# Ending each projection token tile by token tile, in a 256-token, two-block float32 network on one core

## The chip, the cores and the metric

The kernel runs on one core of a Trainium2 chip. TensorE (PE) multiplies, VectorE (DVE) and ScalarE (ACT) do elementwise work, GpSimd (POOL) helps, and SyncE (SP) issues the loads. The metric is the device time of one execution in microseconds (us). Less is better.

## The reference, cut to what matters

Two residual blocks over x of 256 tokens by 2048 features. In each, a mixer and then a gated feed-forward part:

```python
x = x + rms_norm(mix @ w_out[l], post_mix_norm[l])     # "out1" (block 1), "out2" (block 2)
h = rms_norm(x, pre_ffn_norm[l])
u = causal_dwconv(h @ w_up[l], conv_w[l], conv_b[l])   # "up1", "up2"
gate, up = jnp.split(u, 2, axis=-1)
y = (jax.nn.gelu(gate, approximate=True) * up) @ w_down[l]   # "down1", "down2"
x = x + rms_norm(y, post_ffn_norm[l])
```

`rms_norm` divides a token's row by the root of its mean square over all 2048 features. So no part of x can be updated before the last columns of `mix @ w_out` or `y` are known for that token; another token's columns are not needed.

## The kernel before

Tokens lie on the 128 partitions, in two token tiles t = 0, 1. Each matrix product runs over chunks of weights: a chunk is two blocks of 128 rows by 512 columns. Float32 accuracy comes from splitting both operands in a rounded part and a rest: ACT rounds a chunk of `raw` into `whi` (`split_hi`, L213), DVE subtracts into `wlo` (`split_lo`, L218), and PE makes three products a block and token tile, hi by hi, hi by lo, lo by hi (`products`, L231 to L233). There are four slots (RING) for chunks. A slot is reused when PE has used it (`chunk_used`); ACT and DVE work up to three chunks ahead (LEAD), into the next stage too. The stages follow each other as in1, out1, up1, down1, in2, out2, up2, down2. A stage works in groups of 512 output columns; a group fills one of two pairs of PSUM banks (`acc`), one bank a token tile.

In out1, down1, out2 and down2 the stationary operand is the token data (`ahl` or `hhi`, `hlo`), and the moving one is the weights. In up1 and up2 it is turned about (`products_turned`, L251 and L253): the weights are stationary, `ahl` moves in 512 and in 256 columns, and the group takes `acc` or `tp` banks.

At the end of out and down stages stands a chain, the **boundary** in this text: the last group's columns times the gain go to `ybuf` (DVE, `back_group_dve` L396, out stages L1378 and L1919), ACT squares the bank in place with a row sum into `psq` (`back_group_act` L404), DVE adds up the sums and scales (`post_root_dve` L437, L439), ACT takes the root (L421), DVE the reciprocal (L442), DVE updates x by quarters of 512 columns for both token tiles (`add_rows` L450, in quarters q), PE turns x (`pre_pe` L299, eight 128x128 turns a quarter), ACT and DVE split the turned quarter (`pre_act` L306, `pre_dve` L317) into `ahl`, and the next stage's products can start. Every engine takes its instructions in the order in which they are written for it. In SBUF `whi` and `wlo` start 128 bytes past a multiple of 512; `ybuf`, `hhi`, `hlo` and `ahl` start 384 bytes past one.

Of the kernel before, what the change touches and what calls it, by code (L numbers as in the profile page):

```python
# [55 lines left out]
def bass_two_blocks(nc, T):  # L56
    with ExitStack() as ctx:
# [19 lines left out]
        prs = sb("prs", [P, 4, NT])  # L77
        prime = sb("prime", [P, 1])
# [242 lines left out]
        def lead_pe(pe, ph, c, src, ready):  # L321

            for q in {0: (0, 1), 2: (2,), 4: (3,)}.get(c, ()):
                pre_pe(pe, ph, q, src, ready)
# [6 lines left out]
        def lead_dve(dve, ph, c, gain, source):  # L331

            if c == 3:
                source(0)
                source(1)
                pre_dve(dve, ph, 0, gain)
                source(2)
                pre_dve(dve, ph, 1, gain)
            if c == 4:
                source(3)  # L340
# [29 lines left out]
        def back_pe(pe, ph, xhi, xlo, nch, ready=None, ready_count=None, last_count=None, src=None, src_ready=None):  # L370
            def body(i, first):
                for c in range(2 * nch):
                    if c % nch == 0:
                        group(pe, gb[ph] + c // nch + 2 * i)
                    if first:
                        lead_pe(pe, ph, c, src, src_ready)
                    if last_count and CK * c == 4 * (FG - 1):
                        pe.wait_ge(ready, last_count)
                    products(pe, cb[ph] + c + i * (2 * nch), c % RING, acc[(gb[ph] + c // nch) % 2],
                             xhi, xlo, CK * (c % nch), CK * nch, ph if first and c < nch else None)  # L380
            if src is None:
                pe.wait_ge(ready, ready_count)
                with pe.Fori(0, 2) as i:
                    body(i, False)
            else:
                body(0, True)
                body(1, False)
# [22 lines left out]
        def back_act(act, ph, k, nch, last=False):  # L410
            for i in range(2):
                for c in range(LEAD if i else TAIL_HI, 2 * nch):
# [3 lines left out]
                if not (i and last):  # L416
                    for c in range(2 * nch, 2 * nch + LEAD):
                        s_hi(act, ph, i, 2 * nch, c)
                back_group_act(act, ph, k, i, 1)
            act.wait_ge(sem(f"{ph}_post"), 2)  # L420
            act.activation(prs[:, k, :], prs[:, k, :], ACT.Sqrt).then_inc(sem(f"{ph}_post"), 1)  # L421

        def back_dve(dve, ph, k, nch, gain_row, last=False):
            for i in range(2):
                for c in range(LEAD if i else TAIL_LO, 2 * nch):
# [3 lines left out]
                if not (i and last):  # L429
                    for c in range(2 * nch, 2 * nch + LEAD):  # L430
                        s_lo(dve, ph, i, 2 * nch, c)
                back_group_dve(dve, ph, i, 1, nch, gain_row)
            post_root_dve(dve, ph, k)

        def post_root_dve(dve, ph, k):
            dve.wait_ge(group_free, gb[ph] + NG)
            dve.tensor_reduce(prs[:, k, :], psq[:, k, :, :], AX.X, ALU.add).then_inc(sem(f"{ph}_post"), 1)  # L437
            dve.wait_ge(sem(f"{ph}_post"), 1)
            dve.tensor_scalar(prs[:, k, :], prs[:, k, :], 1.0 / D, EPS, ALU.mult, ALU.add)\  # L439
               .then_inc(sem(f"{ph}_post"), 1)  # L440
            dve.wait_ge(sem(f"{ph}_post"), 3)
            dve.reciprocal(prs[:, k, :], prs[:, k, :]).then_inc(sem(f"{ph}_post"), 1)  # L442
            dve.wait_ge(sem(f"{ph}_post"), 4)

        def add_rows(dve, ph, k):

            def add(q):
                c = slice(q * GC, (q + 1) * GC)
                for t in range(NT):
                    dve.scalar_tensor_tensor(out=x[:, t, c], in0=ybuf[:, t, c], scalar=prs[:, k, t:t + 1],  # L450
                                             in1=x[:, t, c], op0=ALU.mult, op1=ALU.add)\
                       .then_inc(sem(f"{ph}_x"), 1)
            return add

        def x_ready(ph):

            def wait(e, q):
                e.wait_ge(sem(f"{ph}_x"), 2 * q + 2)
            return wait
# [351 lines left out]
        def m1_pe(pe):  # L811
# [232 lines left out]
            for n, (g, q) in enumerate(LAID1):  # L1044
# [14 lines left out]
                between(N1 + n)  # L1059

        def m1_act(act):
# [137 lines left out]
            for n in range(LEAD, N1 + len(LAID1) + LEAD):  # L1199
                if n in (3, 6, 8):  # L1200
                    pre_act(act, "in1", n // 3 if n < 8 else 3, 0)
                s_hi(act, "in1", 0, 0, n)
# [7 lines left out]
            back_group_act(act, "out1", 0, 1, 1)  # L1210
            act.wait_ge(sem("out1_post"), 2)
            act.activation(prs[:, 0, :], prs[:, 0, :], ACT.Sqrt).then_inc(sem("out1_post"), 1)

        def m1_dve(dve):
# [208 lines left out]
            for n in range(LEAD, N1 + len(LAID1) + LEAD):  # L1423
# [18 lines left out]
            out1_group(3)  # L1442
            post_root_dve(dve, "out1", 0)
# [62 lines left out]
        def m2_pe(pe):  # L1506
# [80 lines left out]
            for n in range(len(LAID2)):  # L1587
# [12 lines left out]
                between(N2 + n)  # L1600

# [34 lines left out]
        def m2_act(act):  # L1636
# [103 lines left out]
            for n in range(len(LAID2) + LEAD):  # L1740
# [7 lines left out]
                else:  # L1748
                    s_hi(act, "up2", 0, 0, n - len(LAID2))
# [4 lines left out]
            back_group_act(act, "out2", 2, 1, 1)  # L1754
            act.wait_ge(sem("out2_post"), 2)
            act.activation(prs[:, 2, :], prs[:, 2, :], ACT.Sqrt).then_inc(sem("out2_post"), 1)

        def m2_dve(dve):
# [137 lines left out]
            for n in range(len(LAID2) + LEAD):  # L1896
# [5 lines left out]
                if n < len(LAID2):  # L1902
                    s_lo(dve, "out2", 0, 0, n)
                else:
                    s_lo(dve, "up2", 0, 0, n - len(LAID2))
# [4 lines left out]
            out2_group_dve(dve, 3)  # L1910
            post_root_dve(dve, "out2", 2)
# [16 lines left out]
        def _(sp):  # L1928
# [8 lines left out]
            for q in range(4):  # L1937
# [22 lines left out]
        def _(pe):  # L1960
# [3 lines left out]
            back_pe(pe, "down1", hhi, hlo, DCH, sem("up1_hid"), FG, FG + 1)  # L1964
            m2_pe(pe)
            up_pe(pe, "up2", x_ready("out2"))
            back_pe(pe, "down2", hhi, hlo, DCH, sem("up2_hid"), FG, FG + 1)

        @block.scalar
        def _(act):  # L1970
# [3 lines left out]
            back_act(act, "down1", 1, DCH)  # L1974
            m2_act(act)
            up_act(act, "up2", 1, sem("out2_x"), 8)
            back_act(act, "down2", 3, DCH, last=True)

        @block.vector
        def _(dve):  # L1980
# [3 lines left out]
            back_dve(dve, "down1", 1, DCH, gbd)  # L1984
            m2_dve(dve)
            up_dve(dve, "up2", 1, add_rows(dve, "out2", 2))
            back_dve(dve, "down2", 3, DCH, gbd, last=True)
            for q in range(4):
                add_rows(dve, "down2", 3)(q)
# [53 lines left out]
```

## Time and profile before

| | us |
|---|---|
| median of 3 runs | 2558.8 |
| the three runs | 2558.58, 2566.81, 2558.8 |
| profiled execution, its own time | 2559.84 |
| span of the profiled execution | 2557.6 |
| PE busy | 2511.5 (98%) |
| DVE busy | 1653.1 (65%) |
| ACT busy | 1333.7 (52%) |

The span runs from the first to the last instruction; 2.2 us of the execution's time lie around it. PE's busy time counts overlapping matmuls from their modelled ends, so it tells that PE hardly ever waits and not that it works at its peak.

### The profile page before, as it was taken

What the parts mean: (1) busy time and instruction counts of PE and PEld (TensorE: products, weight loads), DVE (VectorE), ACT (ScalarE), POOL (GpSimd) and SP (SyncE); (2) the same over time, 40 slices, a digit from 0 to 9 for tenths busy, and PEclk for the clock granted to TensorE, in tenths of its full rate; (3) what the DMA queues carried; (4) which work ended last, traced back from release to release, by engine and by line L of the source; (5) the groups of instructions that cost most, each with busy time, mean ns of one, the idle gap of its engine ahead of it and who ended that gap; (6) DMA issues with size and microseconds to landing.
All of it is one profiled execution on the core that took longest, in us unless ns stands there. A gap on an engine that the chain in (4) does not pass through costs nothing.

```text
span 2557.6 us, 40519 instructions
## 1 busy us (share of the span) xinstructions
PE 2511.5 (98%) x15344; PEld 2155.9 (84%) x15344; DVE 1653.1 (65%) x2014; ACT 1333.7 (52%) x1749; POOL 222.2 (9%) x94
## 2 busy tenths in 40 slices
PE   8999999999999999999999999999999999999997
PEld 8999877888888888887888888888788888888886
DVE  5665674677677775445485868775676676775444
ACT  5454564656556554444645455554555656554442
POOL 1000000022121211000000000000012131221000
PEclk9999999999999999999999999999999999999999
DMA  7865345566666666665655655546566666656664
GB/s 223 250 205 157 113 127 178 152 190 187 195 190 189 187 191 204 199 191 172 189 174 165 175 157 172 164 145 195 156 181 192 185 186 185 186 181 214 189 190 146
DMA packets 241791, 462.11 MB, mean 181 GB/s; under 512 B 14344, under 2 KB 23361, under 8 KB 241169
## 3 DMA queue, kind: packets, MB, share of 16 engines
q1 hardware_dynamic: 240001, 453.44, 58.7%
q0 software_dynamic: 1568, 7.10, 0.9%
q8 instruction: 77, 1.26, 0.2%
q14 instruction: 33, 0.27, 0.0%
q10 hardware_dynamic: 112, 0.03, 0.0%
HBM read 458.40 MB, written 2.12 MB: 180 GB/s over the span
## 4 chain that ended last, share of the span: by engine, by line
PE 98%; DVE 1%; ACT 1%; issue 0%; DMA 0%; SPq 0%; DVEq 0%; ACTq 0%
PE acc L231 13%; PE acc L233 13%; PE acc L232 13%; PE acc L251 13%; PE tp L251 13%; PE tp L253 7%; PE acc L253 7%; PE acc L828 3%; PE acc L830 2%; PE acc L831 2%; PE acc L1055 1%; PE acc L1057 1%; PE acc L1056 1%; PE tp L299 1%; PE tp L1535 1%; PE acc L836 1%
## 5 line engine op out<-in xcount | busy, mean ns | idle before, releaser
L218 DVE TENSOR_TENSOR wlo<-raw,whi 128x1024 fp32r<-128x1024 f32 x856 | 1070.8, 1258 | 761.6 <-ACT whi L213 759.8
L213 ACT ACTIVATE whi<-raw 128x1024 fp32r<-128x1024 f32 x856 | 903.3, 1059 | 1017.0 <-PE acc L233 467.5
L251 PE MATMUL acc<-ahl,whi 128*128 128x512 f32 x1408 | 495.1, 396 | 0.0
L251 PE MATMUL tp<-ahl,whi 128*128 128x512 f32 x1408 | 494.2, 395 | 0.0
L253 PE MATMUL acc<-ahl,wlo 128*128 128x256 f32 x1408 | 395.0, 281 | 0.0
L253 PE MATMUL tp<-ahl,wlo 128*128 128x256 f32 x1408 | 394.9, 280 | 0.0
L251 PEld LDWEIGHTS acc<-ahl,whi 128*128 128x128 f32 x1408 | 264.3, 188 | 62.3 <-issue 0.4
L251 PEld LDWEIGHTS tp<-ahl,whi 128*128 128x128 f32 x1408 | 263.9, 187 | 61.8
L231 PE MATMUL acc<-whi,ahl 128*128 128x512 f32 x768 | 305.7, 398 | 0.0
L233 PE MATMUL acc<-whi,ahl 128*128 128x512 f32 x768 | 299.9, 390 | 0.0
L232 PE MATMUL acc<-wlo,ahl 128*128 128x512 f32 x768 | 299.5, 390 | 0.0
L232 PE MATMUL acc<-wlo,hhi 128*128 128x512 f32 x704 | 274.0, 389 | 0.0
L231 PE MATMUL acc<-whi,hhi 128*128 128x512 f32 x704 | 274.0, 389 | 0.0
L233 PE MATMUL acc<-whi,hlo 128*128 128x512 f32 x704 | 274.0, 389 | 0.0
L253 PEld LDWEIGHTS acc<-ahl,wlo 128*128 128x128 f32 x1408 | 266.5, 189 | 0.0
L253 PEld LDWEIGHTS tp<-ahl,wlo 128*128 128x128 f32 x1408 | 266.2, 189 | 0.1
L631 POOL TENSOR_TENSOR cvg<-cvg,cvu 128x1024 f32<-128x1024 f32 x22 | 98.0, 4456 | 1516.5 <-DVE cvu L575 1516.5
L233 PEld LDWEIGHTS acc<-whi,ahl 128*128 128x128 f32 x768 | 144.4, 188 | 31.0
L231 PEld LDWEIGHTS acc<-whi,ahl 128*128 128x128 f32 x768 | 144.4, 188 | 29.8 <-issue 0.2
L232 PEld LDWEIGHTS acc<-wlo,ahl 128*128 128x128 f32 x768 | 144.6, 188 | 28.6
L232 PEld LDWEIGHTS acc<-wlo,hhi 128*128 128x128 f32 x704 | 132.1, 188 | 27.6
L233 PEld LDWEIGHTS acc<-whi,hlo 128*128 128x128 f32 x704 | 132.1, 188 | 27.5
(251 smaller groups left out, 2902.5 us busy)
## 6 DMA issues: line engine op xcount, KB each, us to landing
raw<-in_w_up_dram SPq DMA_DIRECT2D x176, 512.0 KB, 4.0
raw<-in_ffn_w_in_dram SPq DMA_DIRECT2D x176, 512.0 KB, 3.8
raw<-in_hgrn_w_in_dram SPq DMA_DIRECT2D x160, 512.0 KB, 3.6
raw<-in_w_in_dram SPq DMA_DIRECT2D x88, 512.0 KB, 3.7
raw<-in_w_down_dram SPq DMA_DIRECT2D x88, 512.0 KB, 3.9
raw<-in_ffn_w_out_dram SPq DMA_DIRECT2D x88, 512.0 KB, 3.7
raw<-in_w_out_dram SPq DMA_DIRECT2D x32, 512.0 KB, 3.7
raw<-in_hgrn_w_out_dram SPq DMA_DIRECT2D x32, 512.0 KB, 3.9
```

Of the source, the lines that this page charges most:

```text
L213: act.activation(whi[:, s, :], raw[:, s, :], ACT.Copy).then_inc(hi_done, 1)
L218: dve.tensor_tensor(wlo[:, s, :], raw[:, s, :], whi[:, s, :].bitcast(F32), ALU.subtract).then_inc(lo_done, 1)
L231: pe.matmul(out[:, t, :], xh, whi[:, s, c], start=(kt == 0), stop=False)
L232: pe.matmul(out[:, t, :], xh, wlo[:, s, c], start=False, stop=False)
L233: mm = pe.matmul(out[:, t, :], xl, whi[:, s, c], start=False, stop=(kt == nk - 1))
L251: pe.matmul(o[:, ct % 2, :].rearrange("p (a t) -> p a t", a=2), whi[:, s, c], ahl[:, :, kt, :], start=(kt == 0), stop=False, skip_group_ch ...
L253: mm = pe.matmul(o[:, ct % 2, 0:S], wlo[:, s, c], ahi[:, kt, :], start=False, stop=(kt == KT - 1), skip_group_check=True)
L299: mm = pe.transpose(tp[q % 2][:, k, t * P:(t + 1) * P], src[:, t, c:c + P], ident[:, :])
L631: pool.tensor_tensor(cvg[:, :, :], cvg[:, :, :], cvu[:, :, :], ALU.mult).then_inc(sem(f"{ph}_pr"), 1)
L828: pe.matmul(o[:, d], whi[:, s, a], ahi[:, kt, :], start=first and ct % 2 == 0, stop=False, skip_group_check=True)
L830: pe.matmul(o[:, d], whi[:, s, a], alo[:, kt, :], start=False, stop=False, skip_group_check=True)
L831: mm = pe.matmul(o[:, d], wlo[:, s, a], ahi[:, kt, :], start=False, stop=last, skip_group_check=True)
```

## The change

Four edits, at all four boundaries.

1. The last four chunks of an out or down stage are multiplied for token tile 0 first and then for tile 1 (`last_products`); a semaphore `token0` tells when tile 0 is whole. `back_pe` is written out where it was a loop of two passes.
2. Norm and additions go by token tile. DVE sums the squares of the first three groups ahead (`rest_dve`), ACT squares a tile's last 512 columns out of the bank into the other pair of banks and takes the root with scale and bias in the same instruction (`last_act`), DVE makes the reciprocal, then updates x a quarter and tile at a time, with the last group's `ybuf` (`last_y`) and two chunks of `wlo` of the next stage in between (`last_dve`). The three `whi` of the next stage stand between tile 0 and tile 1 on ACT.
3. PE turns quarters 0 and 1 of x by token tile (`pre_pe_by_token`), and in up1 and up2 ahead of the wait for the banks. After down2 the output goes out as one transfer for tile 0 and four for tile 1.
4. A tensor `rest` (32 bytes a partition) and 96 bytes of padding come in, so that `ybuf`, `hhi`, `hlo` and `ahl` start at a multiple of 512 bytes. `whi` and `wlo` stay 128 bytes past one.

```diff
+        rest = sb("rest", [P, 4, NT])
+        sb("pad128", [P, 24])
...
+        def pre_pe_by_token(pe, ph, src, ready):
+
+            for t in range(NT):
+                for q in range(2):
+                    ready(pe, q, t)
+                    for k in range(4):
+                        c = (4 * q + k) * P
+                        mm = pe.transpose(tp[q][:, k, t * P:(t + 1) * P], src[:, t, c:c + P], ident[:, :])
+                    if t == NT - 1:
+                        mm.then_inc(sem("pre_turned"), 1)
...
             if c == 3:
-                source(0)
-                source(1)
                 pre_dve(dve, ph, 0, gain)
-                source(2)
+                s_lo(dve, ph, 0, 0, 2)
+                for t in range(NT):
+                    source(2, t)
                 pre_dve(dve, ph, 1, gain)
...
+        def last_products(pe, ph, k, n, xhi, xlo, kts):
+
+            out = acc[(gb[ph] + NG - 1) % 2]
+            for t in range(NT):
+                for j in range(RING):
+                    if t == 0:
+                        pe.wait_ge(lo_done, n + j + 1)
+                    s = (n + j) % RING
+                    for kk in range(CK):
+                        kt, c = kts[j] + kk, slice(kk * GC, (kk + 1) * GC)
+                        xh, xl = xhi[:, kt, t * P:(t + 1) * P], xlo[:, kt, t * P:(t + 1) * P]
+                        pe.matmul(out[:, t, :], xh, whi[:, s, c], start=False, stop=False)
+                        pe.matmul(out[:, t, :], xh, wlo[:, s, c], start=False, stop=False)
+                        mm = pe.matmul(out[:, t, :], xl, whi[:, s, c], start=False, stop=(j == RING - 1 and kk == CK - 1))
+                    if t:
+                        mm.then_inc(chunk_used, 1)
+                if t == 0:
+                    mm.then_inc(sem("token0"), 1)
+
+        def last_act(act, ph, k, t, end):
...
+            act.activation(other[:, t, :], a[:, t, :], ACT.Square, accum_out=psq[:, k, t, NG - 1:NG])\
+               .then_inc(sem("last_sq"), 1)
+            act.wait_ge(sem("last_sq"), NT * k + t + 1)
+            act.wait_ge(sem("rest"), 2 * k + 2)
+            act.activation(prs[:, k, t:t + 1], psq[:, k, t, NG - 1:NG], ACT.Sqrt, scale=1.0 / D,
+                           bias=rest[:, k, t:t + 1]).then_inc(sem("post_root"), 1)
...
+        def last_dve(dve, ph, k, gain_row, nxt):
+
+            add = add_rows(dve, ph, k)
+            unroot_dve(dve, ph, k, 0)
+            add(0, 0)
+            last_y(dve, ph, k, 0, gain_row)
+            s_lo(dve, nxt, 0, 0, 0)
+            add(1, 0)
+            s_lo(dve, nxt, 0, 0, 1)
+            unroot_dve(dve, ph, k, 1)
+            add(0, 1)
+            last_y(dve, ph, k, 1, gain_row)
+            add(1, 1)
...
+            last_act(act, ph, k, 0, cb[ph] + 4 * nch)
+            if nxt:
+                for c in range(LEAD):
+                    s_hi(act, nxt, 0, 0, c)
+            last_act(act, ph, k, 1, cb[ph] + 4 * nch)
...
+                for t in range(NT):
+                    unroot_dve(dve, ph, k, t)
+                    add_rows(dve, ph, k)(0, t)
+                    last_y(dve, ph, k, t, gain_row)
+                    for q in range(1, NG):
+                        add_rows(dve, ph, k)(q, t)
...
-                    if first and c == 0:
-                        pe.wait_ge(group_free, gb[ph])
-                    elif c % CPG == 0 and not first:
+                    if c % CPG == 0 and not first:
                         group(pe, gb[ph] + c // CPG + i * 2)
                     if first:
                         lead_pe(pe, ph, c, x, src_ready)
+                    if first and c == 0:
+                        pe.wait_ge(group_free, gb[ph])
...
+            sp.wait_ge(sem("down2_x"), NG)
+            sp.dma_start(T["out"][0][0:P, :], x[:, 0, :]).then_inc(sem("out"), 16)
+            for q in range(NG):
                 c = slice(q * GC, (q + 1) * GC)
-                sp.wait_ge(sem("down2_x"), 2 * q + 2)
-                sp.dma_start(T["out"][0][:, c].rearrange("(n p) c -> p n c", p=P), x[:, :, c]).then_inc(sem("out"), 16)
-            sp.wait_ge(sem("out"), 64)
+                sp.wait_ge(sem("down2_x"), NG + q + 1)
+                sp.dma_start(T["out"][0][P:S, c], x[:, 1, c]).then_inc(sem("out"), 16)
+            sp.wait_ge(sem("out"), 16 * (NG + 1))
```

VectorE at the end of down1, before. L396 makes `ybuf`, L450 updates x, L317 splits the turned x:

```order
L218 TENSOR_TENSOR wlo<-raw,whi 128x1024 [waits hi_done] x21
L396 TENSOR_TENSOR ybuf<-acc,gbd 128x512 [waits chunk_used,down1_gain]
L396 TENSOR_TENSOR ybuf<-acc,gbd 128x512
L437 TENSOR_REDUCE prs<-psq 128x2 [waits group_free]
L439 TENSOR_SCALAR prs<-prs 128x2 [waits down1_post]
L442 RECIPROCAL prs<-prs 128x2 [waits down1_post]
L450 SCALAR_TENSOR_TENSOR x<-ybuf,prs,x 128x512 [waits down1_post]
L450 SCALAR_TENSOR_TENSOR x<-ybuf,prs,x 128x512 x3
L317 SCALAR_TENSOR_TENSOR ahl<-tp,gains,ahl 128x256 [waits pre_hi] x4
```

The same place in the changed kernel (L530 is the update of x, L431 `ybuf`, L220 `wlo`, L330 the split of x):

```order
L220 TENSOR_TENSOR wlo<-raw,whi 128x1024 [waits hi_done] x14
L437 RECIPROCAL prs<-prs 128x1 [waits post_root]
L530 SCALAR_TENSOR_TENSOR x<-ybuf,prs,x 128x512 [waits post_rs]
L431 TENSOR_TENSOR ybuf<-acc,gbd 128x512 [waits last_sq,down1_gain]
L220 TENSOR_TENSOR wlo<-raw,whi 128x1024 [waits hi_done]
L530 SCALAR_TENSOR_TENSOR x<-ybuf,prs,x 128x512
L220 TENSOR_TENSOR wlo<-raw,whi 128x1024 [waits hi_done]
L437 RECIPROCAL prs<-prs 128x1 [waits post_root]
L530 SCALAR_TENSOR_TENSOR x<-ybuf,prs,x 128x512 [waits post_rs]
L431 TENSOR_TENSOR ybuf<-acc,gbd 128x512 [waits last_sq,down1_gain]
L530 SCALAR_TENSOR_TENSOR x<-ybuf,prs,x 128x512
L330 SCALAR_TENSOR_TENSOR ahl<-tp,gains,ahl 128x256 [waits pre_hi] x4
```

The second reciprocal has only one update of x behind it before PE can turn tile 1's first quarter, where one reciprocal had two; but two splits of weights now stand in this row.

ScalarE at the same place, before (L404 squares, L421 is the root with the load of its table, L306 splits x):

```order
L213 ACTIVATE whi<-raw 128x1024 [waits chunk_used,landed2]
L404 ACTIVATE acc,psq<-acc 128x512 [waits down1_y]
L404 ACTIVATE acc,psq<-acc 128x512
L421 ACT_TABLE_LOAD
L421 ACTIVATE prs<-prs 128x2 [waits down1_post]
L306 ACTIVATE ahl<-tp,gains 128x256 [waits pre_turned]
```

and in the changed kernel (L412 squares, L416 is the root, L215 `whi`):

```order
L412 ACTIVATE acc,psq<-acc 128x512 [waits token0]
L416 ACT_TABLE_LOAD [waits rest]
L416 ACTIVATE prs<-psq,rest 128x1 [waits last_sq]
L215 ACTIVATE whi<-raw 128x1024 [waits chunk_used,landed0]
L215 ACTIVATE whi<-raw 128x1024 [waits chunk_used,landed1]
L215 ACTIVATE whi<-raw 128x1024 [waits chunk_used,landed2]
L412 ACTIVATE acc,psq<-acc 128x512 [waits chunk_used]
L416 ACTIVATE prs<-psq,rest 128x1 [waits rest,last_sq]
L319 ACTIVATE ahl<-tp,gains 128x256 [waits pre_turned]
```

The square no longer waits for DVE's `ybuf`, the table load stands with tile 0, and the three `whi` have moved behind tile 0's root.

## Rows read from the trace of the kernel before

**Rows 1.** The page: its first line and the chain that ended last.
```profile
span 2557.6 us, 40519 instructions
PE 98%; DVE 1%; ACT 1%; issue 0%; DMA 0%; SPq 0%; DVEq 0%; ACTq 0%
```

**Rows 2.** PE's waits: us in total, times, longest us.
```profile
PE tp L299 <- DVE x L450: 16.3, 3, 6.0
...
PE acc L1055 <- DVE ahl L1369: 2.8, 1, 2.8
```

**Rows 3.** Timeline, end of down1 to in2's first product: start us, us, engine.
```profile
1192.18 0.39 PE L233 MATMUL acc<-whi,hlo 128*128 128x512 f32 x1
1192.67 1.29 DVE L396 TENSOR_TENSOR ybuf<-acc,gbd 128x512 f32<-128x512 f32 x2 [0.41 <-PE acc L233]
1193.99 0.58 ACT L404 ACTIVATE acc<-acc 128x512 f32<-128x512 f32 x1 [2.99 <-DVE ybuf L396]
...
1195.30 1.28 ACT L421 ACT_TABLE_LOAD   x1
...
1196.59 0.20 ACT L421 ACTIVATE prs<-prs 128x2 f32<-128x2 f32 x1
...
1197.03 2.74 DVE L450 SCALAR_TENSOR_TENSOR x<-ybuf,prs,x 128x512 f32<-128x512 f32 x4
...
1198.59 3.65 PE L299 MATMUL tp<-ident,x 128*128 128x128 f32 x16 [6.02 <-DVE x L450]
1200.57 3.27 ACT L306 ACTIVATE ahl<-tp,gains 128x256 fp32r<-128x256 f32 x8 [3.77 <-PE tp L299]
1201.44 1.66 DVE L317 SCALAR_TENSOR_TENSOR ahl<-tp,gains,ahl 128x256 fp32r<-128x256 f32 x4 [1.67 <-ACT ahl L306]
...
1202.07 0.77 PE L231 MATMUL acc<-whi,ahl 128*128 128x512 f32 x1
```

**Rows 4.** Timeline, out1's last product and up1's first (out2 to up2 alike).
```profile
452.70 0.39 PE L1057 MATMUL acc<-whi,ahl 128*128 128x512 f32 x1
...
461.71 0.77 PE L251 MATMUL acc<-ahl,whi 128*128 128x512 f32 x1
```

**Rows 5.** The page's groups: count, then busy us, mean ns.
```profile
L218 DVE TENSOR_TENSOR wlo<-raw,whi 128x1024 fp32r<-128x1024 f32 x856 | 1070.8, 1258 | 761.6 <-ACT whi L213 759.8
L213 ACT ACTIVATE whi<-raw 128x1024 fp32r<-128x1024 f32 x856 | 903.3, 1059 | 1017.0 <-PE acc L233 467.5
L251 PE MATMUL acc<-ahl,whi 128*128 128x512 f32 x1408 | 495.1, 396 | 0.0
...
L231 PE MATMUL acc<-whi,ahl 128*128 128x512 f32 x768 | 305.7, 398 | 0.0
...
L231 PE MATMUL acc<-whi,hhi 128*128 128x512 f32 x704 | 274.0, 389 | 0.0
```

**Rows 6.** Windows: length, then busy us (count) of PE, PEld, DVE, ACT, POOL, PEclk.
```profile
970.00:1180.00 210.00, 210.00 (x928) 173.88 (x928) 100.75 (x84) 85.39 (x90) 9.97 (x4) 1.00 0.64 198
```

**Rows 7.** Timeline of the end of down2, and a window of the output's transfer (last column GB/s).
```profile
2544.02 0.39 PE L233 MATMUL acc<-whi,hlo 128*128 128x512 f32 x1
...
2548.87 5.39 DVE L450 SCALAR_TENSOR_TENSOR x<-ybuf,prs,x 128x512 f32<-128x512 f32 x8
...
2552.30:2553.30 1.00, 0.00 (x0) 0.00 (x0) 1.00 (x2) 0.00 (x0) 0.00 (x0) 0.50 1.02 377
```

**Rows 8.** Windows with PE's clock at half: behind L1055's wait, up1's and in2's start.
```profile
398.70:402.10 3.40, 3.40 (x10) 2.66 (x9) 0.00 (x0) 0.00 (x0) 0.00 (x0) 0.51 0.40 146
...
461.70:463.50 1.80, 1.80 (x6) 1.57 (x6) 1.80 (x5) 1.66 (x6) 0.00 (x0) 0.50 0.00 0
...
1202.00:1204.20 2.20, 2.20 (x7) 1.78 (x6) 2.20 (x5) 2.06 (x6) 0.00 (x0) 0.50 0.00 0
```

**Rows 9.** Windows of 400 us inside up1 and inside up2.
```profile
500.00:900.00 400.00, 400.00 (x2310) 352.71 (x2309) 286.77 (x343) 236.97 (x280) 85.06 (x27) 1.00 0.63 189
1850.00:2250.00 400.00, 400.00 (x2266) 346.88 (x2265) 276.53 (x332) 230.67 (x276) 86.92 (x27) 1.00 0.62 186
```

More of the change, by code:

```diff
@@ L372, in body, with back_pe @@
+        def back_pe(pe, ph, k, nch, ready):
+            pe.wait_ge(ready, FG)
+            for i in range(2):
                 for c in range(2 * nch):
@@ L374, in body @@
                         group(pe, gb[ph] + c // nch + 2 * i)
[L375 to L387, printed above, removed]
+                    if CK * c == 4 * (FG - 1) and not i:
+                        pe.wait_ge(ready, FG + 1)
+                    if not i or c < 2 * nch - RING:
+                        products(pe, cb[ph] + c + i * (2 * nch), c % RING, acc[(gb[ph] + c // nch) % 2],
+                                 hhi, hlo, CK * (c % nch), CK * nch)
+            last_products(pe, ph, k, cb[ph] + 4 * nch - RING, hhi, hlo, [CK * (nch - RING + j) for j in range(RING)])
         def back_group_dve(dve, ph, i, gg, nch, gain_row):
@@ L415, in back_act, with back_dve @@
                         back_group_act(act, ph, k, i, 0)
[L416 to L423, printed above, removed]
+                if not i:
+                    back_group_act(act, ph, k, i, 1)
+            last_act(act, ph, k, 0, cb[ph] + 4 * nch)
[3 more added lines that the diff above has]
+            last_act(act, ph, k, 1, cb[ph] + 4 * nch)
+        def back_dve(dve, ph, k, nch, gain_row, nxt):
             for i in range(2):
-                for c in range(LEAD if i else TAIL_LO, 2 * nch):
+                for c in range(LEAD if i else TAIL_LO, 2 * nch + (0 if i else LEAD)):
                     s_lo(dve, ph, i, 2 * nch, c)
@@ L428, in back_dve @@
                         back_group_dve(dve, ph, i, 0, nch, gain_row)
[L429 to L443, printed above, removed]
+                    if i and c == nch + 7:
+                        rest_dve(dve, ph, k)
@@ L445, in add_rows, with add @@
+                if not i:
+                    back_group_dve(dve, ph, i, 1, nch, gain_row)
+            if nxt:
+                last_dve(dve, ph, k, gain_row, nxt)
+            else:
+                for t in range(NT):
+                    unroot_dve(dve, ph, k, t)
[3 more added lines that the diff above has]
+                        add_rows(dve, ph, k)(q, t)
         def add_rows(dve, ph, k):
-            def add(q):
+            def add(q, t):
@@ L448, in add @@
                 c = slice(q * GC, (q + 1) * GC)
[L449 to L452, printed above, removed]
+                if q == NG - 1 and t == 0:
+                    dve.wait_ge(sem(f"{ph}_y"), NT * (NG - 1) + 1)
+                if q == NG - 1 and t == 1:
+                    dve.wait_ge(group_free, gb[ph] + NG)
@@ L1585, in m2_pe @@
                 between(n)
-            for n in range(len(LAID2)):
+            for n in range(len(LAID2) - RING):
                 if n == 0:
@@ L1894, in m2_dve @@
                 between(n)
-            for n in range(len(LAID2) + LEAD):
+            for n in range(len(LAID2)):
                 if n in (3, 4, 5, 6):
@@ L1901, in m2_dve @@
                     out2_pre_dve(dve, n - 6)
[L1902 to L1905, printed above, removed]
+                s_lo(dve, "out2", 0, 0, n)
                 between(N2 + n)
@@ L1963, in _ @@
             up_pe(pe, "up1", x_ready("out1"))
-            back_pe(pe, "down1", hhi, hlo, DCH, sem("up1_hid"), FG, FG + 1)
+            back_pe(pe, "down1", 1, DCH, sem("up1_hid"))
             m2_pe(pe)
             up_pe(pe, "up2", x_ready("out2"))
-            back_pe(pe, "down2", hhi, hlo, DCH, sem("up2_hid"), FG, FG + 1)
+            back_pe(pe, "down2", 3, DCH, sem("up2_hid"))
         @block.scalar
@@ L1973, in _ @@
             up_act(act, "up1", 0, sem("out1_x"), 8)
-            back_act(act, "down1", 1, DCH)
+            back_act(act, "down1", 1, DCH, "in2")
             m2_act(act)
             up_act(act, "up2", 1, sem("out2_x"), 8)
-            back_act(act, "down2", 3, DCH, last=True)
+            back_act(act, "down2", 3, DCH, None)
         @block.vector
@@ L1983, in _ @@
             up_dve(dve, "up1", 0, add_rows(dve, "out1", 0))
-            back_dve(dve, "down1", 1, DCH, gbd)
+            back_dve(dve, "down1", 1, DCH, gbd, "in2")
             m2_dve(dve)
             up_dve(dve, "up2", 1, add_rows(dve, "out2", 2))
-            back_dve(dve, "down2", 3, DCH, gbd, last=True)
-            for q in range(4):
-                add_rows(dve, "down2", 3)(q)
+            back_dve(dve, "down2", 3, DCH, gbd, None)
 _INS = ["x", "pre_mix_norm", "w_in", "lambda_q1", "lambda_k1", "lambda_q2", "lambda_k2", "diff_subln", "cmp_pos_k",
```

68 lines of the change are left out of this document (47 added, 21 removed).

## The prediction, made before the changed kernel ran

> **What bounds the kernel now.** I read the page first. The span is 2557.6 us and PE holds 98% of the chain that ended last [rows 1]. So only two kinds of thing can change the time: gaps on PE, and the spacing of its matmuls. PE's own waits come next. The largest is one line at three places, the turns of x waiting for the update of x, 16.3 us [rows 2]. That is what edits 1 to 3 touch. The fourth place has no PE work behind it: the tail after down2.
>
> The timeline of one boundary [rows 3] shows the chain. Call L the start of the last product, 1192.18. At L+0.49 DVE starts `ybuf` (two tiles, 1.29). At L+1.81 ACT squares (the pair lasts to the table load, 1.31), then loads the root's table for 1.28; the root takes 0.20; x is updated from L+4.85. The turns start at L+6.41, the first split of turned x on DVE at L+9.26, and the first product at L+9.89. At the end of out1 the same stretch takes 9.01 [rows 4]; what is missing there is the table load. The end of out2 reads like it, to 0.01 us. In the tail the eight updates run from L+4.85 to L+10.24 (0.67 each), and the span ends at L+13.6 [rows 1, 7].
>
> **The change part by part, in time from L.** PE's total of matmuls is the same. Reordered, the last four chunks are two passes of 24 matmuls. In down1 928 matmuls start in 210 us, 0.226 each [rows 6], so a pass is 5.4 us and tile 0 is whole at L−5.4.
>
> *Does tile 0's pass wait for weights?* It wants the fourth chunk's `wlo` 18 matmuls after it starts, 4.1 us. ACT frees that slot's predecessor 0.5 after the pass starts, then 1.06 for `whi` and 1.26 for `wlo` [rows 5]: about 2.8 us with the hand-over. There is 1.3 us to spare, so I cost the reordering at nothing. If ACT or DVE were held up longer than that, PE would stop for the difference.
>
> *ACT.* Tile 0: square from L−4.95 to −4.3 (0.66, half of the pair), table load 1.28, root: done at −2.75 (out stages: −4.0, no load). Then three `whi`, each when tile 1's pass has used a slot (−3.6, −2.2, −0.9): after down1 they end at −1.6, −0.6 and +0.5. Tile 1's square starts at +0.5 either way, as early as the data allows. Root at 1.45. The squaring no longer waits 1.3 for `ybuf`, and 1.28 of table load has moved behind matmuls.
>
> *DVE after down1.* Reciprocal at −2.7, update (0,0) −2.5 to −1.8, `ybuf` to −1.1, `wlo` to 0.1, update (1,0) to 0.8, `wlo` to 2.0. Tile 1's root was ready at 1.45, so here the queue is 0.5 late: the two splits of weights now cost this much. Reciprocal, then update (0,1) 2.2 to 2.9, `ybuf` to 3.55, update (1,1) to 4.25. In the out stages all of tile 0 and both `wlo` are done by 0.75, so update (0,1) follows the root, 1.7 to 2.4, and (1,1) ends at 3.75.
>
> *PE.* Tile 0's eight turns go right behind the last product. Tile 1's first four start at 3.0 after down1 (2.5 after out) and take 0.44 at full clock. Square and copy latencies are those of rows 3: last turn to first ACT split 0.49, to DVE's split 0.87 more, to the first product 0.63 more. That gives 5.3 after down1 and 4.8 after out, against 9.89 and 9.01. Tile 1's second four turns (at 4.4, 3.9) fit in before. Gains: **4.6**, and **4.2** twice.
>
> *Behind the restart.* DVE now makes the third `wlo`, update 2 and the split of quarter 1 behind the first split: `wlo` at 7.0, quarter 2 of x at 8.4, quarter 1 of `ahl` at 10.1. PE wants them from about 10.4 on. Covered by a few tenths to 2 us; without the cover each restart would lose that back.
>
> *Tail.* There are no `whi` or `wlo` to make. Tile 0's x is whole at L+0.9; tile 1's runs 1.7 to 5.1. Before, 3.3 us passed from the last update to the end of the span; that gives 8.4. The transfer moves 377 GB/s [rows 7], 5.6 us for 2.1 MB, and before took 7.4 from its first ready quarter (L+6.2) to the end; from 0.9 on that gives 8.3. Both agree: gain 13.6 − 8.4 = **5.2**.
>
> *Clock.* PE's clock fell to half at the boundaries, and up1 and in2 ran their first 1.8 and 2.2 us of products at it [rows 8], losing 0.9 and 1.1; up2 lost nothing. After the change PE is idle for less, but in bits. A wait of 2.8 us [rows 2] was followed by 3.4 us at half clock [rows 8], so a fall stays likely. Bounds: nothing, or 3.4 us of products at half clock at each restart, 1.7. I take 1.0 at each of three, since the fall can come anywhere in between: 3.0 against 2.0 now, **a loss of 1.0**.
>
> *Addresses.* `ahl`, `hhi` and `hlo` move from 384 to 0 past a multiple of 512. Does any row show a start to matter? In down1 the moving `whi` starts at 128, spacing 226 ns: 13 ns above 512 columns at 2.4 GHz. In up1 the moving `ahl` starts at 384, and 1155 pairs of 512 and 256 columns take 400 us [rows 9]: 346 ns a pair, 26 above, again 13 a matmul. Two starts, one overhead. I cost edit 4 at nothing, with both signs open.
>
> By the Trainium skill ("TensorE: Matmul & The Clock Gate", section Back-to-back issue gap) the fixed part is 2.5 ns, and this trace shows 13. If the starting address were what makes the difference, the sum would gain 11 ns on each of 5,632 matmuls with `ahl` moving, 62 us more; an estimate from that page, and no row supports it.
>
> *Sum.* 4.2 + 4.6 + 4.2 + 5.2 − 1.0 = 17.2 us off the profiled execution's own 2559.8 is 2542.6. That execution lies 1.0 above the median of the runs, so **2541.6**. What is uncertain in it (half clock already during the turns, 0.4 a boundary; the clock's bounds, −3.0 to +2.1; hand-overs of 0.05) gives its own range of 2538 to 2546.
>
> **The rivals.** *The spacing in up1 and up2.* The same instructions take 346.3 ns a pair in up1 and 353.1 in up2 (1133 pairs in 400 us) [rows 9]. A stage has 1,408 pairs (that count for `acc` and the same for `tp` over two stages [rows 5]), nearly all in the steady part, so one stage at the longer spacing costs 9 us. Nothing is written differently in the two, so I read it as a state that a stage falls into at its start. The three runs, 2558.6, 2558.8 and 2566.8, lie 8 us apart, which would be one more stage at the long spacing. The change shifts both starts and an address, so both short gives 2541.6 − 9 = **2532.6**, both long **2550.7**. For one of each speaks that it is what is seen most; against, that nothing shows what sets it.
>
> *The queue behind the restart is late.* If DVE's splits come 2 us late at each restart (ACT's and DVE's hand-overs longer, half clock in the turns), 6 us are given back: **2547.6**. Against: the cover above.
>
> *The address slows matmuls.* This is the case that ends slower. The step seen between the two stages is 3.4 ns a matmul. If a start at 0 caused it on up1's 2,816 matmuls (9.6 us) and on the 4,416 with 512 columns of the other stages (three lines of 768 and 704 [rows 5], 15.0 us), and half as much again on the rest, the sum is 2541.6 + 29 = **2571**. It decides from 17.2 us, or 2.4 ns on each of the 7,232. Against: two different starts, one overhead.
>
> *The address causes the overhead.* If a start at 0 took away all 13 ns a matmul where `ahl` moves, 5,632 matmuls give 73 us: 2541.6 − 73 = **2469**. Against: the same. It is the case that the page's rule in the part on addresses stands for.
>
> *Nothing is gained*: it would need the first product to wait for something that the change does not bring forward. The last product's data, 0.5 + 0.66 + 0.2 + 0.2 + 0.7 + turns and splits 2.4, is the shortest chain, 4.7, and lies well under 9; I see no such thing except by both of the first two rivals together (2556.7).
>
> **How the numbers follow.** Likeliest case 0.53; both short 0.16; both long 0.15; queue late 0.08; both long and queue late (within 0.3%) 0.03; slower by address 0.04; overhead gone 0.01. 0.3% is 7.7 us, about what a measurement of this kernel can tell from no change. So faster 0.93, same 0.03, slower 0.04. The range takes in the first four cases nearly whole: 2532 to 2551.
>
> **What would show it.** The first product 4.8 us after the last of out1 and out2, and 5.3 after down1's; PE's waits for x near 2 us each; the table load of down1 some 4 us before L; the span ending 8.4 us after down2's last product; 400 us inside up1 and up2 holding 2310 or 2266 matmuls. The prediction is wrong if the two windows hold another count than these, if PE waits for `wlo` or `ahl` within 12 us behind a restart, or if it waits in the pass of tile 0.

## The result: slower, and the profile after

The changed kernel takes 2568.4 us, median of 20 runs (2566.6 to 2571.6), against 2558.3 for the kernel before in 20 runs (2549.0 to 2567.4). The ratio is 1.0041, 95% interval 1.0029 to 1.0053. Forecast were 2541.6 us and a range up to 2551. The kernel is some 10 us slower where 17 us less were forecast.

PE's waits in the changed kernel (us in total, times, longest) answer to [rows 2]:

```profile
PE tp L311 <- DVE x L530: 5.6, 6, 1.3
PE acc L1135 <- DVE ahl L1450: 2.8, 1, 2.8
```

The wait for the update of x is down from 16.3 us at three places to 5.6 at six. So the edits at the boundaries work. The timeline from the end of down1 to the first product of in2, for [rows 3]:

```profile
1195.75 1.28 ACT L416 ACT_TABLE_LOAD   x1
...
1197.24 3.11 ACT L215 ACTIVATE whi<-raw 128x1024 fp32r<-128x1024 f32 x3
...
1197.57 0.75 DVE L530 SCALAR_TENSOR_TENSOR x<-ybuf,prs,x 128x512 f32<-128x512 f32 x1
1198.24 0.68 DVE L431 TENSOR_TENSOR ybuf<-acc,gbd 128x512 f32<-128x512 f32 x1
1198.84 1.21 DVE L220 TENSOR_TENSOR wlo<-raw,whi 128x1024 fp32r<-128x1024 f32 x1
...
1200.19 0.40 PE L399 MATMUL acc<-whi,hlo 128*128 128x512 f32 x1
...
1200.42 1.03 PE L311 MATMUL tp<-ident,x 128*128 128x128 f32 x8
...
1201.96 0.75 DVE L530 SCALAR_TENSOR_TENSOR x<-ybuf,prs,x 128x512 f32<-128x512 f32 x1
...
1202.77 0.65 PE L311 MATMUL tp<-ident,x 128*128 128x128 f32 x4 [1.31 <-DVE x L530]
...
1204.96 0.77 PE L233 MATMUL acc<-whi,ahl 128*128 128x512 f32 x1
```

The last product starts at 1200.19 and the first of the next stage at 1204.96: 4.8 us, where it was 9.9. The table load and tile 0's first update of x lie ahead of the last product. The same gap is 4.7 us behind out1 and behind out2, where it was 9.0. The last products and the first ones, then down2's last product:

```profile
453.74 0.39 PE L399 MATMUL acc<-whi,ahl 128*128 128x512 f32 x1
...
458.42 0.47 PE L253 MATMUL acc<-ahl,whi 128*128 128x512 f32 x1 [0.28 <-DVE ahl L330]
...
1810.35 0.39 PE L399 MATMUL acc<-whi,ahl 128*128 128x512 f32 x1
...
1815.02 0.77 PE L253 MATMUL acc<-ahl,whi 128*128 128x512 f32 x1 [0.28 <-DVE ahl L330]
...
2558.30 0.40 PE L399 MATMUL acc<-whi,hlo 128*128 128x512 f32 x1
```

The tail from down2's last product to the end of the span is 7.9 us, where it was 13.6. Together **19.5 us less** in the gaps.

What took that and more shows in windows inside the stages. The rows answer to [rows 6, 9]. Columns are the window, its length, then busy us and count of PE, PEld (the loads of the stationary operand), DVE, ACT and POOL, PE's clock, the DMA share and GB/s.

```profile
500.00:900.00 400.00, 400.00 (x2281) 350.59 (x2280) 279.83 (x334) 233.44 (x277) 86.06 (x27) 1.00 0.63 187
970.00:1180.00 210.00, 210.00 (x906) 170.24 (x905) 99.26 (x90) 83.03 (x88) 10.11 (x4) 1.00 0.58 194
1850.00:2250.00 400.00, 400.00 (x2281) 350.58 (x2280) 279.51 (x339) 234.88 (x278) 85.61 (x27) 1.00 0.63 187
```

In down1 906 matmuls fit into 210 us where 928 did. PE never waits there and its clock is whole in both. By start-to-start times, a 512-column matmul takes 232.4 ns in place of 226.7 (a window's count takes in one or two that are under way at its edge, so it reads some 0.5 ns less). In up a pair of 512 and 256 columns takes 351.1 ns in both stages, where it was 346.7 in up1 and 353.3 in up2.

The account of the two profiled spans, 2557.6 and 2566.2, from the first product of one stage to the last product of the next boundary:

| stretch | before | after | difference |
|---|---|---|---|
| start to out1's last product | 452.70 | 453.74 | +1.0 |
| up1 and down1 | 730.5 | 741.8 | +11.3 |
| in2 and out2 | 594.2 | 605.4 | +11.2 |
| up2 and down2 | 738.7 | 743.3 | +4.6 |
| three boundaries | 27.9 | 14.1 | −13.8 |
| tail | 13.6 | 7.9 | −5.7 |

The sum is +8.6, the difference of the spans (up2 was at its longer spacing before, so it lost less). Every stretch with matmuls is longer, the ones with token-wise code as well as those whose code is untouched.

### The profile page after: what moved, and what is told of

The parts are those of the page before. It is cut to its first block, busy times and chain, and to the rows that moved or that the text cites. A ratio compares the mean times of both kernels' runs of the same rounds, so it can differ in the third digit from the quotient of the medians.

```text
span 2566.2 us, 40354 instructions
## 1 busy us (share of the span) xinstructions
PE 2535.9 (99%) x15344; PEld 2158.6 (84%) x15344; DVE 1649.4 (64%) x2018; ACT 1335.3 (52%) x1753; POOL 222.7 (9%) x94
## 4 chain that ended last, share of the span: by engine, by line
PE 98%; DVE 1%; issue 0%; ACT 0%; DMA 0%; SPq 0%; DVEq 0%; ACTq 0%
PE acc L233 13%; PE acc L234 13%; PE acc L235 13%; PE acc L253 13%; PE tp L253 13%; PE acc L255 7%; PE tp L255 7%; PE acc L908 2%; PE acc L910 2%; PE acc L911 2%; PE acc L1135 1%; PE acc L1137 1%; PE acc L1136 1%; PE tp L1617 1%; PE acc L916 1%; PE acc L918 1%
## 5 line engine op out<-in xcount | busy, mean ns | idle before, releaser
L220 DVE TENSOR_TENSOR wlo<-raw,whi 128x1024 fp32r<-128x1024 f32 x856 | 1067.5, 1254 | 774.9 <-ACT whi L215 774.0
L215 ACT ACTIVATE whi<-raw 128x1024 fp32r<-128x1024 f32 x856 | 903.0, 1059 | 1030.5 <-PE acc L235 481.8
L233 PE MATMUL acc<-whi,hhi 128*128 128x512 f32 x672 | 265.1, 395 | 0.0
L234 PE MATMUL acc<-wlo,hhi 128*128 128x512 f32 x672 | 265.1, 395 | 0.0
L235 PE MATMUL acc<-whi,hlo 128*128 128x512 f32 x672 | 265.1, 395 | 0.0
L908 PE MATMUL acc<-ahl,whi 128*128 128x256 f32 x512 | 151.1, 295 | 1.6 <-DVE ahl L330 1.6
L235 PEld LDWEIGHTS acc<-whi,hlo 128*128 128x128 f32 x672 | 126.6, 188 | 29.7
```

The source lines that it names most:

```text
L215: act.activation(whi[:, s, :], raw[:, s, :], ACT.Copy).then_inc(hi_done, 1)
L220: dve.tensor_tensor(wlo[:, s, :], raw[:, s, :], whi[:, s, :].bitcast(F32), ALU.subtract).then_inc(lo_done, 1)
L233: pe.matmul(out[:, t, :], xh, whi[:, s, c], start=(kt == 0), stop=False)
L234: pe.matmul(out[:, t, :], xh, wlo[:, s, c], start=False, stop=False)
L235: mm = pe.matmul(out[:, t, :], xl, whi[:, s, c], start=False, stop=(kt == nk - 1))
L908: pe.matmul(o[:, d], whi[:, s, a], ahi[:, kt, :], start=first and ct % 2 == 0, stop=False, skip_group_check=True)
```

## The experiments

Theories after the result: **distance** or **start**, that the new SBUF addresses slow the matmuls, by the operands' distance from each other or by one operand's own start; **order**, that the products' new order and the code written out where it was a loop do. `whi` and `wlo` always start in one place modulo 512, and `ybuf`, `hhi`, `hlo` and `ahl` in another, common one, unless said. The distance below is that of `hhi`, `hlo` and `ahl` from `whi`, modulo 512.

### pad384: the changed kernel at the old addresses

```diff
-        sb("pad128", [P, 24])
+        sb("pad128", [P, 120])
```

> The changed kernel with the padding at 480 bytes in place of 96, so that ybuf, hhi, hlo and ahl start 384 bytes past a multiple of 512 again, as before the change. Address theory: the spacing of 512-column matmuls in down1 goes from 232.4 back to 226.7 ns, up1 and up2 take 346.7 or 353.3 ns a pair in place of 351.2, and only the gains at the four boundaries are left (4.3 + 5.1 + 4.3 + 5.7 = 19.4 us by the two traces): about 2539 us, with steps of 9 us up or down between runs. Rival, the written-out order (the two passes of down are no loop any more, the code is longer) slows PE: 232.4 ns stays and the time is 2568 us.

```profile
500.00:900.00 400.00, 400.00 (x2310) 352.69 (x2309) 286.99 (x343) 237.12 (x280) 85.04 (x27) 1.00 0.63 189
970.00:1180.00 210.00, 210.00 (x929) 173.87 (x928) 99.06 (x85) 84.28 (x89) 4.60 (x3) 1.00 0.60 199
```

Measured: 2532.4 us (2528.3 to 2538.1), before beside it 2549.7, ratio 0.9928 (0.9911 to 0.9945). All spacings are those of before. In this profile both up stages have the short one. The gaps stay at 4.7, 4.9 and 4.7 us and the tail at 8.0. With 384 bytes more of padding the change brings 17 us, and the order theory falls: the order of the products and the written-out code are those of the changed kernel.

### before0: the kernel before at the new addresses

```diff
         prs = sb("prs", [P, 4, NT])
+        sb("pad128", [P, 32])
         prime = sb("prime", [P, 1])
```

> The kernel before with 128 bytes of padding and nothing else, so that ybuf, hhi, hlo and ahl start at a multiple of 512. Address theory: 232.4 ns in down1 and 351.2 ns a pair in up, so 2568.4 + 19.4 = 2588 us, and no 9 us steps between runs. Rival, the written-out order: 2558 us, nothing changed.

```profile
970.00:1180.00 210.00, 210.00 (x905) 170.25 (x905) 100.13 (x90) 85.46 (x92) 10.11 (x4) 1.00 0.61 193
```

Measured: 2587.6 us (2585.1 to 2588.9), ratio 1.0141 (1.0120 to 1.0161). One line that computes nothing costs some 29 us against the middle level of before. Beside it, before was at 2549.7, with nine of eleven runs at its lowest level; against that it is 38 us. The two factors add: 2587.6 − 2568.4 = 19.2 us is what the token-wise boundaries bring at these addresses too.

### both128 and pad256: own start or distance?

In both128 `raw`, `whi`, `wlo` and x move by 128 bytes and `rest` goes behind `ahl`:

```diff
+        sb("shift", [P, 32])
         raw = sb("raw", [P, RING, CK * GC])
...
-        rest = sb("rest", [P, 4, NT])
-        sb("pad128", [P, 24])
...
             ahi, alo = ahl[:, 0, :, :], ahl[:, 1, :, :]
+            rest = sb("rest", [P, 4, NT], where=r)
```

> The changed kernel with raw, whi, wlo and x moved up by 128 bytes (whi and wlo 256 past a multiple of 512) and ybuf, hhi, hlo and ahl at 0, rest laid behind ahl. The distance between the two operands of a matmul modulo 512 is 256, as in the kernel before; the second operand's own start is 0, as in the changed kernel. Theory 'distance': 226.7 ns in down1 and about 2539 us. Theory 'own start at 0 is slow': 232.4 ns and 2568 us. A third value would say that whi's own start counts too.

In pad256 the padding is `[P, 88]`:

> The changed kernel with 352 bytes of padding: ybuf, hhi, hlo and ahl 256 bytes past a multiple of 512, whi and wlo at 128, distance 128. Theory 'own start at 0 is slow': 226.7 ns in down1, 2539 us. Theory 'distance': distance 256 was fast and 384 slow; 128 is the mirror of 384, so if only the size of the gap to the nearer multiple counts it is slow too, 232.4 ns and 2568 us.

First both128, then pad256:

```profile
970.00:1180.00 210.00, 210.00 (x928) 173.91 (x927) 98.94 (x85) 83.77 (x88) 3.96 (x3) 1.00 0.60 199
1850.00:2250.00 400.00, 400.00 (x2267) 346.91 (x2266) 278.26 (x338) 230.82 (x273) 86.90 (x27) 1.00 0.63 186
```

```profile
970.00:1180.00 210.00, 210.00 (x905) 170.27 (x904) 99.73 (x91) 83.35 (x88) 10.11 (x4) 1.00 0.57 193
```

Measured: both128 2534.6 us (ratio 0.9931, 0.9906 to 0.9956); pad256 2567.9 us (1.0064, 1.0044 to 1.0084). `ahl`, `hhi` and `hlo` start at 0 in both128 and in the changed kernel, and one is fast and the other slow. `whi` starts at 128 in pad384 and in pad256, and again one is fast and the other slow. So neither operand's own start decides; the distance fits all of them. both128's second row shows up2 at the long spacing, in that execution.

### pad128, pad0 and pad448: which distances?

The padding is `[P, 56]`, none at all, and `[P, 8]`.

> The changed kernel with 224 bytes of padding: ybuf, hhi, hlo and ahl start 128 past a multiple of 512, as whi and wlo do, distance 0. So far distance 256 gave 226.7 ns and distances 128 and 384 gave 232.4. If two reads that start in the same place of 512 bytes meet most, distance 0 is at least as slow as 384: 232.4 ns or more, 2568 us or more. If instead only 128-byte multiples that are odd are slow (the two reads then out of step by half of 256), distance 0 is fast: 226.7 ns and 2530 to 2539 us.

> The changed kernel without the padding: the 32 bytes of rest alone move ybuf, hhi, hlo and ahl to 416 past a multiple of 512, distance 288. If the distance counts in steps of 128 or more, it behaves like 256: 226.7 ns, 2530 to 2539 us. If it counts finely, the spacing lies between 226.7 and 232.4, 1.4 ns up for a quarter of the way, about 2545 us.

> The changed kernel with 32 bytes of padding: ybuf, hhi, hlo and ahl at 448, distance 320 from whi, that is 64 past a multiple of 256. Seen so far: 0 past a multiple of 256 gives 226.7 ns in down1, 32 past it 233.3, 128 past it 232.4. Theory 'only multiples of 256 are fast': 232 to 234 ns, 2555 to 2570 us. Rival: a pattern finer than that, with 64 fast: 226.7 ns, 2530 us.

pad128, then pad0 (two windows), then pad448 (two):

```profile
970.00:1180.00 210.00, 210.00 (x928) 173.91 (x927) 98.81 (x85) 83.77 (x88) 3.80 (x3) 1.00 0.60 199
```

```profile
500.00:900.00 400.00, 400.00 (x2310) 354.61 (x2309) 286.73 (x342) 237.18 (x281) 85.02 (x27) 1.00 0.63 189
970.00:1180.00 210.00, 210.00 (x902) 169.06 (x901) 96.03 (x84) 82.76 (x87) 3.84 (x2) 1.00 0.58 193
```

```profile
500.00:900.00 400.00, 400.00 (x2266) 348.31 (x2266) 278.10 (x333) 230.74 (x275) 86.88 (x27) 1.00 0.62 186
970.00:1180.00 210.00, 210.00 (x902) 169.39 (x900) 99.95 (x92) 82.84 (x87) 10.17 (x4) 1.00 0.58 193
```

| distance | kernels | 512 columns, down1, ns | pair in up, ns |
|---|---|---|---|
| 0 | pad128, best | 226.7 | 346.7 in these traces |
| 256 | before, pad384, both128 | 226.7 | 346.7 or 353.3 |
| 288 (256 + 32) | pad0 | 233.3 | 346.7 |
| 320 (256 + 64) | pad448 | 233.3 | 353.3 |
| 384 (256 + 128) | after, before0 | 232.4 | 351.1 (351.5 in up2 of before0) |
| 128 | pad256 | 232.4 | 351.1 |

Measured: pad128 2530.0 us in two runs; pad0 2555.6 in eight (2555.0 to 2556.9), ratio 0.9989 (0.9967 to 1.0012); pad448 2574.6 in the profiled run. pad448's other run took 4164.5 us at a mean granted clock of 0.556, where the first had 0.997; it tells nothing of the distance, and why the clock stayed down in it is open. Where the 512 columns are weights and the stationary operand is token data, only the multiples of 256 were fast of the six distances tried. In pad0 I had expected a value between, and the spacing was already at its highest. The pairs of up follow the distance otherwise: 288 is as fast as any there. Without any padding the change would just have kept even with before.

### ahl0: only one of the operands moved

`rest` goes behind `ahl` as in both128, there is no `shift` and no padding, and

```diff
-        sb("hold2", [P, NT * D + 2 * FT * S + 512])
+        sb("hold2", [P, NT * D + 2 * FT * S + 512 + 32])
```

> The changed kernel with rest behind ahl, no padding, and 128 bytes ahead of ahl alone: hhi and hlo stay at distance 256 from whi, ahl is at distance 384. Distance theory, matmul by matmul: down1 and down2, which read hhi and hlo, keep 226.7 ns, while out and in2 take 232.4 and up 351.2 ns a pair. Time: 2532.4 or more by in2 and out (2,688 matmuls by 5.7 ns, 15.3 us) and by up (4.5 ns on 1,408 pairs a stage where it was short, 12.7 us), about 2557 us; the two downs give back 12 us against the changed kernel's 2568. Rival: ybuf, x or the other tensors that moved cause it; then down1 differs too or nothing does.

```profile
500.00:900.00 400.00, 400.00 (x2280) 350.58 (x2279) 279.67 (x334) 233.65 (x278) 86.11 (x27) 1.00 0.63 186
970.00:1180.00 210.00, 210.00 (x928) 173.90 (x927) 102.36 (x90) 84.84 (x89) 9.97 (x4) 1.00 0.60 199
```

Measured: 2555.1 us (2554.8 to 2557.5), 2557 expected. up, which reads `ahl`, is slow (351.1 ns a pair), and down1, which reads `hhi` and `hlo`, is fast (226.7 ns), in one kernel. `ybuf` and x lie where they lay before the change in it, so they are not the cause: the distance acts matmul by matmul, by the two operands that PE reads.

### bankfirst: the turns behind the bank wait again

At distance 256, in `up_pe` the wait on `group_free` stands ahead of `lead_pe`, as before the change.

```diff
+                    if first and c == 0:
+                        pe.wait_ge(group_free, gb[ph])
-                    if c % CPG == 0 and not first:
+                    elif c % CPG == 0 and not first:
                         group(pe, gb[ph] + c // CPG + i * 2)
                     if first:
                         lead_pe(pe, ph, c, x, src_ready)
-                    if first and c == 0:
-                        pe.wait_ge(group_free, gb[ph])
```

> The changed kernel with 480 bytes of padding (distance 256) and with the wait for the banks ahead of the turns of x again in up1 and up2. The bank is free when tile 1's ybuf has been made, about 3.1 us after the last product, so all sixteen turns start there and the first product of up comes 6.4 us after the last of out in place of 4.68; in2 keeps 4.91. Theory that this edit carries its share: 1.7 us at each of two stages, 3.4 us over pad384. Rival: the turns of tile 0 are hidden anyway and nothing changes, 4.68.

Its timeline behind out1:

```profile
452.34 0.39 PE L399 MATMUL acc<-whi,ahl 128*128 128x512 f32 x1
...
455.42 3.11 PE L311 MATMUL tp<-ident,x 128*128 128x128 f32 x16 [2.69 <-DVE ybuf L431]
...
459.22 0.76 PE L253 MATMUL acc<-ahl,whi 128*128 128x512 f32 x1 [0.69 <-DVE ahl L330]
```

Measured: 2543.8 us (2535.1 to 2554.8), ratio 0.9951 (0.9929 to 0.9973), against 2532.4 for pad384. All sixteen turns start 3.1 us after the last product, as expected. The first product comes 6.9 us (out1) and 7.4 us (out2) after the last, against 4.7: 5.0 us together where 3.4 were expected. The turns themselves take 3.11 us for 16 where eight take 1.03 in the changed kernel; the clock was at half from 456.1 for 6.8 us, so the idle stretch costs twice.

The medians are 11 us apart, but they come from two series of runs, with before at 2549.7 beside pad384 and at 2558.0 beside bankfirst; by the ratios it is some 6 us, and their intervals overlap. The traces are clearer. bankfirst's span is 15.8 us longer than pad384's: about 5.0 are the gaps, 9.4 are up2, long here (2267 matmuls in its window) and short in pad384's, and 1.8 are half clock in up1's first 3.7 us of products, where pad384's trace has none. both128's trace has bankfirst's spacings and 3.4 us of products at half clock; against its span of 2537.1 us bankfirst's 2542.0 is 4.9 more, the gaps alone.

### chunkwise: token tiles behind, but not in the products

At distance 256, the last four chunks are multiplied with both tiles in turn (the loop over t inside the one over j), so that tile 0 is whole 1.4 us ahead of the last product.

```diff
-            for t in range(NT):
-                for j in range(RING):
-                    if t == 0:
-                        pe.wait_ge(lo_done, n + j + 1)
-                    s = (n + j) % RING
+            for j in range(RING):
+                pe.wait_ge(lo_done, n + j + 1)
+                s = (n + j) % RING
+                for t in range(NT):
...
-                if t == 0:
-                    mm.then_inc(sem("token0"), 1)
+                    elif j == RING - 1:
+                        mm.then_inc(sem("token0"), 1)
```

> pad384 (distance 256) with the last four chunks multiplied chunk by chunk again, both token tiles of a chunk in turn; everything behind it by token tile as before. Tile 0 is then whole 1.4 us before the last product in place of 5.4. Theory that the token pass carries the gain: ACT squares tile 0 at L-0.9, makes the three whi of the next stage behind it (3.2 us) and only then squares tile 1, so the first product of the next stage comes 7.4 us after the last one behind out (4.68 in pad384), 8.8 behind down1 with the table load (4.91), and the tail takes about 11 us in place of 8.0: some 12.7 us over pad384, 2543 to 2551 us. Rival: finer norm and additions alone pay, and the gaps stay under 6 us.

Behind out1:

```profile
452.06 0.58 ACT L411 ACTIVATE acc<-acc 128x512 f32<-128x512 f32 x1 [8.40 <-PE acc L398]
...
452.98 2.93 ACT L215 ACTIVATE whi<-raw 128x1024 fp32r<-128x1024 f32 x3
452.99 0.39 PE L398 MATMUL acc<-whi,ahl 128*128 128x512 f32 x1
...
455.81 0.58 ACT L411 ACTIVATE acc<-acc 128x512 f32<-128x512 f32 x1
...
461.16 0.77 PE L253 MATMUL acc<-ahl,whi 128*128 128x512 f32 x1 [0.28 <-DVE ahl L330]
```

Measured: 2549.7 us (2548.6 to 2566.6), ratio 0.9996 (0.9979 to 1.0014). The gaps are 8.2, 9.5 and 8.0 us and the tail 12.1, close to before: 15.5 us more than pad384 in its trace, where 12.7 were expected. The three `whi` stand between the two squares on ACT: tile 1 could be squared 0.5 after the last product and is squared 2.8 after it. So this kernel's finer norm and additions carry almost nothing without the order of the products: its gaps and tail are together 3.8 us shorter than before's, but its clock is at half in the first 2.7, 3.2 and 4.6 us of products behind the restarts, which costs some 3 us more than in before's trace. What the order of the products is worth by itself is not shown for the three boundaries, since up to 2.3 of the 3.5 us lost behind out1 are tile 1's square waiting for the three `whi`; a kernel with the `whi` behind both squares was not run. In the tail there are no `whi`, and the order is worth 4.1 of the 5.6 us there (13.6 before, 12.1 here, 8.0 in pad384).

### best: a version that beats both

The same kernel as pad128, in more runs.

> The same kernel as pad128 (distance 0, 224 bytes of padding), timed in more rounds as the version that beats both kernels. Theory 'the distance modulo 256 is all that counts': as pad384, 2528 to 2540 us with steps of some 9 us for an up stage at the long spacing, ratio to before 0.989 to 0.993. Rival: distance 0 is free of the long spacing, and all runs lie at 2527 to 2533.

Measured: 2531.9 us (2528.6 to 2538.2), ratio 0.9924 (0.9903 to 0.9945), no different from pad384. At distance 0 the times still spread: two of six lie above 2537, 9 us over the fastest, as one up stage at the long spacing would have it, though no trace at distance 0 shows one.

## Why the prediction was wrong

**The step that failed is edit 4, costed at nothing.** The argument was "two starts, one overhead": moving `whi` from 128 in down1, moving `ahl` from 384 in up1, both 13 ns above their columns. But the other operand of the first was at 384, of the second at 128. Both comparisons have the distance 256. The two rows varied everything but the quantity that decides, so they could not show that addresses are free. The experiments put in its place, at distance 384: 5.7 ns more for each 512-column matmul with weights moving (down, in2, out), and 4.4 ns more for a pair of up where it was short, 2.2 less where it was long. On the 4,416 matmuls of the rival below and one up stage of each kind that is 25.2 + 3.1 = 28.3 us, an estimate from these spacings without out1's matmuls; the stretches of products grew by 28.0, 0.9 of it by the clock. The mean overhead of up's pairs, 13 ns a matmul, also hid that its two matmuls are not alike: in pad384's trace the next one starts 16.7 ns late behind 512 columns and 10.0 behind 256.

**The slower rival** had the right tensors and almost the right time, 2571 us against 2568.4, and only 0.04 of the chance. The time was luck. Its cause was a start at 0, which both128 (start 0, fast) and pad256 (start 256, slow) disprove. Its step of 3.4 ns was that between up1 and up2, two stages at the same addresses. It gave the down, in2 and out stages 15.0 us, where 25.2 act, and up 14 us (4.4 of them for "the rest", with no working), where 3.1 act. Its break-even point (17.2 us) was right and was passed.

**The boundaries**, edits 1 to 3, were right. Predicted gaps were 4.8, 5.3 and 4.8 us, measured 4.7, 4.8 and 4.7; the tail 8.4 against 7.9. Gain 19.5 us against 18.2. in2's gap came out half a microsecond short of the forecast since DVE's queue is hardly late: its second `wlo` (from 1200.64, 1.22 us long) ended just as tile 1's root was ready, and the reciprocal started at 1201.77, 1.6 us after the last product where 2.0 were forecast. That tile 0's pass doesn't wait for weights was right too. So was that nothing waits behind the restart: PE's 0.6 us for `ahl` are the last part of the gaps themselves, 0.28 ahead of each first product of up1 and up2. Of the signs of being wrong, one came true, the count of matmuls in the windows, and it is the sign of the addresses. pad384 confirms the sum without edit 4: 17.3 us less than before beside it, where 17.2 were forecast. Its 2532.4 us are below the 2541.6 forecast since before was at 2549.7 beside it, and not at 2558.

**The clock**: its loss of 1.0 was about right as a sum. It was forecast as 1.0 at each of three restarts. Half clock fell on in2's first 2.4 us and up2's first 3.4 us of products, none in up1; 2.9 us lost against 2.0 before:

```profile
1204.96:1207.40 2.44, 2.44 (x7) 1.96 (x7) 2.44 (x5) 2.29 (x6) 0.00 (x0) 0.50 0.94 388
1815.02:1818.40 3.38, 3.38 (x11) 2.90 (x12) 3.38 (x6) 2.47 (x6) 0.00 (x0) 0.50 0.05 7
```

That the sum fits is partly luck: in pad384's trace, with the same boundaries, the clock was whole at all three restarts and nothing was lost.

**The spacing of up** as a state was right for distance 256: the 20 runs of before lie at three levels, 3 near 2549, 11 near 2558, 6 near 2567, as zero, one or two stages at 353.3 ns would have it. At distance 384 the spacing is 351.1 to 351.5 ns in every trace and the runs lack these levels. So what the changed kernel loses depends on before's level: 10 us against the middle one, 19 against a before with both stages short. What sets the state stays open; no experiment was made on it.

## What to carry to other kernels

Where PE never waits, the spacing of its matmuls is a term of its own. With any edit that moves a tensor, even padding, count the matmuls in a window of each stage, before and after. To show that an address doesn't matter, vary the distance between the two operands that PE reads, not only each start; here 256 bytes against 384 was worth 1.1% of the whole time. Work behind a reduction can be hidden by finishing one token tile early. It takes the order of the products for it, and a place for long instructions in the closing engine's queue where they hold up neither tile; how the gain divides between the two is shown only for the tail.

## What the runs showed that I had not expected

- The spacing of 512-column float32r matmuls in down1 is 226.7 ns at distance 0 and 256, 233.3 at 288 and 320, 232.4 at 128 and 384, at full clock and with no wait on PE. The pairs of up, with token data moving, take 346.7 to 353.3 ns and order the distances differently (288 is fast there). Why is open.
- At the best distance a matmul here starts 13 ns later than the columns of the one ahead of it account for at 2.4 GHz: every 226.7 ns with 512 columns in down1, every 120 ns with 256 columns in in1. The Trainium skill ("TensorE: Matmul & The Clock Gate", section Back-to-back issue gap) gives 2.5 ns for the fixed part of an isolated matmul's gap at full clock; no distance that was tried came near it.
- An idle stretch of PE cost again in the clock: sixteen turns took 3.11 us after a wait of 2.69 us (bankfirst), where the first eight took 1.03 us right behind products (after).
